# RWKV scan: the triangular inverse of a 64-step chunk in seven products, two small VectorE steps in GpSimd's queue

## The reference, cut to what matters

```
for each head, direction and chunk:   (I - A) s = x
A  = strictly triangular 64x64 product of decayed keys, scaled by 1 / |k|^2
y  = decayed r S + masked products with v and s;   S = decayed S + k^T v + b^T s
```

## Time and profile before

| what | value |
|---|---|
| median of 3 runs | 4044.05 us |
| range of the runs | 4041.13 to 4046.62 us |
| span of the profiled execution | 4039.7 us |
| TensorE busy in the span | 3727.0 us (92%) |
| VectorE, ScalarE, GpSimd busy | 2360.8, 1204.0, 1321.7 us |

### The profile page before, as it was taken

The page is one execution under the profiler, slowest core; times in us unless marked ns, Lnnn a source line. Parts: engine busy times, 40 slices in busy tenths (PEclk is TensorE's granted clock), DMA queues, the critical chain, the costliest instruction groups (busy, mean ns, idle before and its releaser), DMA issues. The chain is left out here.

```text
span 4039.7 us, 81581 instructions
## 1 busy us (share of the span) xinstructions
PE 3727.0 (92%) x32706; PEld 2683.2 (66%) x32706; DVE 2360.8 (58%) x3864; ACT 1204.0 (30%) x2668; POOL 1321.7 (33%) x1020
## 2 busy tenths in 40 slices
PE   8888999898999999899999997998999999899887
PEld 6667878657787898777344444874999998733333
DVE  4568882545985445565444445767888776623333
ACT  3352222344222322331111112224455454111112
POOL 4443444434445364573000000431555453000000
PEclk9999999999999999999999999999999999899999
DMA  4114542303554122345999995356333234589997
GB/s 128 56 53 170 184 157 93 104 1 105 178 187 146 66 96 75 99 138 228 404 420 420 420 420 212 134 177 201 88 89 91 78 93 147 199 366 422 421 421 316
DMA packets 231204, 787.80 MB, mean 195 GB/s; under 512 B 56008, under 2 KB 64024, under 8 KB 171136
## 3 DMA queue, kind: packets, MB, share of 16 engines
q1 hardware_dynamic: 225008, 764.12, 50.9%
q0 software_dynamic: 5328, 19.40, 1.2%
q10 hardware_dynamic: 576, 0.09, 0.0%
HBM read 736.15 MB, written 47.38 MB: 194 GB/s over the span
## 5 line engine op out<-in xcount | busy, mean ns | idle before, releaser
L2887 POOL DMA_INDIRECT moe0e_xg<-moe_h,moe_first_rows x20 | 18.9, 947 | 546.3 <-DVE moe_first_rows L3044 540.5
L3011 ACT ACT_TABLE_LOAD x32 | 41.1, 1283 | 519.2 <-PE moe1e_p_u L2957 262.4
L373 POOL TENSOR_TENSOR gmi_w_lo<-gmi_rows_w,gmi_w_hi 128x512 fp32r<-128x512 f32 x64 | 120.2, 1878 | 159.8 <-ACT gmi_w_hi L415 159.8
L3960 PE MATMUL scan_bank<-scan_T,scan_off 64*64 64x64 f32 x3840 | 159.4, 220 | 8.5 <-issue 5.7
L373 POOL TENSOR_TENSOR p_w_lo<-p_rows_w,p_w_hi 128x512 fp32r<-128x512 f32 (+3 forms) x88 | 113.5, 1291 | 159.9 <-ACT p_w_hi L415 159.9
L2887 POOL DMA_INDIRECT moe1e_xg<-moe_h,moe_first_rows x17 | 16.0, 940 | 451.0 <-DVE moe_first_rows L3044 444.4
L1159 POOL TENSOR_TENSOR f0u_w_lo<-f0u_w,f0u_w_hi 128x1024 fp32r<-128x1024 f32 x42 | 115.0, 2757 | 137.6 <-ACT f0u_w_hi L1175 137.6
L1159 POOL TENSOR_TENSOR f1u_w_lo<-f1u_w,f1u_w_hi 128x1024 fp32r<-128x1024 f32 x42 | 114.3, 2742 | 137.5 <-ACT f1u_w_hi L1175 137.5
L1227 DVE SCALAR_TENSOR_TENSOR f0u_ada<-hT,condition,f0u_ada 128x512 f32<-128x512 f32 x168 | 148.2, 949 | 16.4 <-DMA hT<-in_ada_w_dram 15.9
L1227 DVE SCALAR_TENSOR_TENSOR f1u_ada<-hT,condition,f1u_ada 128x512 f32<-128x512 f32 x168 | 140.5, 903 | 20.5 <-DMA hT<-in_ada_w_dram 20.0
L2984 PE MATMUL moe0e_p_y<-moe_ring,moe0e_gatedT 128*64 128x512 f32 x608 | 137.6, 605 | 7.8 <-ACT moe0e_gatedT L3013 7.8
(11 more groups left out here) (903 smaller groups left out, 11529.7 us busy)
## 6 DMA issues: line engine op xcount, KB each, us to landing
moe_ring<-in_moe_w_down_dram SPq DMA_DIRECT2D x140, 1024.0 KB, 18.0
gm_uT<-in_moe_w_gu_dram SPq DMA_DIRECT2D x111, 1024.0 KB, 16.6
moe_ring<-in_moe_w_gu_dram SPq DMA_DIRECT2D x102, 1024.0 KB, 24.7
walk_memory<-in_moe_w_gu_dram SPq DMA_DIRECT2D x60, 1024.0 KB, 24.4
hT<-in_ada_w_dram SPq DMA_DIRECT2D x48, 1024.0 KB, 6.8
f0u_w<-in_ffn_w_gate_up_dram SPq DMA_DIRECT2D x22, 1024.0 KB, 4.8
f1u_w<-in_ffn_w_gate_up_dram SPq DMA_DIRECT2D x22, 1024.0 KB, 4.8
gmi_rows_w<-in_ga_w_in_dram SPq DMA_DIRECT2D x64, 256.0 KB, 2.7
```

The costliest lines, as they stand in the source:

```text
L373: nc.gpsimd.tensor_tensor(w_lo[t % 2][:, 0:width], w[t % RAW][:, 0:width], w_hi[t % 2][:, 0:width], ALU.subtract).then_inc(w_lo_made, 1)
L2887: pool.indirect_dma_start(xg[:], None, H.h, bass.IndirectOffsetOnAxis(rows[:, 0:1], 0)).then_inc(gathered, 16)
L3011: nc.scalar.activation(sg[:], p_g[:], ACT.Silu).then_inc(silu_ready, 1)
L3960: mm = nc.tensor.matmul(out[r], lhsT[r], rhs[r], start=start, stop=stop, skip_group_check=True)
```

## The change

The inverse is reorganised. A 64x64 triangle consists of two 32x32 blocks on the diagonal and a piece that joins them. Inside the blocks R is now built as (I + W^8)(I + W^4)(I + W^2)(I + W) times the first join, W being a product of the remaining joins with that first inverse. Since R is then zero outside the two diagonal blocks, its 64 columns are added ("folded") to 32, and the power W (64 columns) and the folded R (32 columns) lie side by side in `WR`, so that one matmul of 96 columns gives both the square and the product.

There are PRODUCTS = 7 stages of 3 group products: FIRST (64 columns), three squaring stages (96 columns), LAST_POWER (32 columns, the folded R alone), OUTER and FINAL (64 columns) for the outer join. `UNITS` lists 30 units: a squaring product is two units of half a group each, the others are one unit each. The walk parts and the factor steps are placed on units as they were on group products.

GpSimd's queue is now, per head: for each group `full` and `off`, then three folds (128x128), three outer pieces, `split_block`, `add_shift`, the factors `km` and `kh`, and then three unfolds (`r_full`, 128x256, which wait for VectorE's LAST_POWER additions), and `eed`. VectorE gives up `split_block` and `add_shift`.

```diff
-LEVELS = 5
+BLOCK_BITS = 5
+PRODUCTS = 7
...
+    FIRST, LAST_POWER, OUTER, FINAL = 0, 4, 5, 6
+    UNITS = [(n, part) for n in range(NI) for part in ((0, 4),) * (n // NG not in (1, 2, 3)) + ((0, 2), (2, 4)) * (n // NG in (1, 2, 3))]
...
-        off = [sb(f"off{n}", [P, 4, CH]) for n in range(NZ)]
-        Z = [sb(f"Z{n}", [P, 4, CH]) for n in range(2)]
+        off, off_outer = (sb(n, [P, STEPS, CH]) for n in ("off", "off_outer"))
+        Z = sb("Z", [P, STEPS, CH])
+        WR = sb("WR", [P, STEPS, CH + CH // 2])
+        full = sb("full", [P, STEPS, CH])
...
@@ gpsimd @@
-                    for n in range(NZ):
...
-                        nc.gpsimd.tensor_tensor(off[n][:], strict(u, g), over4(join[:, l + 1, :]), ALU.mult).then_inc(s["off_ready"], 1)
+                        nc.gpsimd.tensor_tensor(full[:, g4, :], strict(u, g), over4(join[:, 0, :]), ALU.mult).then_inc(s["r_joined"], 1)
+                        nc.gpsimd.tensor_tensor(off[:, g4, :], strict(u, g), over4(join[:, 1, :]), ALU.mult).then_inc(s["off_ready"], 1)
+                    for g in range(NG):
+                        g4 = slice(4 * g, 4 * g + 4)
+                        pool.wait_ge(s["r_ready"], h * NG + g + 1)
+                        nc.gpsimd.tensor_tensor(WR[:, g4, folded], full[:, g4, 0:CH // 2], full[:, g4, CH // 2:CH], ALU.add).then_inc(s["r_folded"], 1)
+                    for g in range(NG):
+                        nc.gpsimd.tensor_tensor(off_outer[:, 4 * g:4 * g + 4, :], strict(u, g), over4(join[:, 2, :]), ALU.mult).then_inc(s["outer_ready"], 1)
+                    split_block(h)
+                    add_shift(h)
                     if ahead is not None:
                         factors(ahead)
+                    for g in range(NG):
+                        g4 = slice(4 * g, 4 * g + 4)
+                        pool.wait_ge(s["r_added"], h * ADDED + adds_through(LAST_POWER * NG + g))
+                        nc.gpsimd.tensor_tensor(by_block(full[:, g4, :]), WR[:, g4, folded].rearrange("p c (o t) -> p c o t", o=1).broadcast_to([P, 4, 2, CH // 2]),
+                                                join[:, 3, :].rearrange("p (q o t) -> p q o t", q=1, o=2).broadcast_to([P, 4, 2, CH // 2]), ALU.mult).then_inc(s["r_full"], 1)
+                    if ahead is not None:
+                        end_decays(ahead)
@@ scalar @@
+                    for k, (n, (first, end)) in enumerate(UNITS):
+                        if n // NG in (FIRST, OUTER):
+                            copy_z(n)
+                        if squares(n) and end == 4:
+                            copy_power(n)
+                        walk_part(walk, k - 1)
+                        if ahead is not None and k % 2 == 0 and k:
+                            factor_part(ahead, k // 2 - 1)
@@ vector @@
                     add_bonus()
-                    split_block()
-                    add_shift()
...
+                    for k, (n, (first, end)) in enumerate(UNITS):
+                        if end == 4:
+                            if n and squares(n - 1):
+                                add_product(n - 1)
+                                turn_product(n - 1)
+                            if not squares(n):
+                                add_product(n)
+                            if n and not squares(n - 1):
+                                turn_product(n - 1)
                         if ahead is not None:
+                            factor_part(fc, ahead, k)
@@ tensor @@
+                        for q in range(first, end):
+                            j = n % NG * 4 + q
+                            if stage == FIRST or stage == OUTER:
+                                mm = mmul(one(n)[:, q, :], stationary[:, j, :], T[:, j, :])
+                            elif squares(n):
+                                mm = mmul(wide(n)[:, q], stationary[:, j, :], WR[:, j, :])
+                            elif stage == LAST_POWER:
+                                mm = mmul(narrow(n)[:, q, :], stationary[:, j, :], WR[:, j, folded])
+                            else:
+                                mm = mmul(one(n)[:, q, :], stationary[:, j, :], full[:, j, :])
...
+                    for k, (n, (first, end)) in enumerate(UNITS):
+                        product(n, first, end)
+                        walk_part(k - 1)
```

More of the change, by code:

```diff
@@ new lines, in turn, with add_product @@
+                    def turn(out, of):
+                        V.transpose(out, of).then_inc(s["t_made"], 1)
+                    def add_product(n):
+                        g4 = chunks(n)
+                        if n // NG == FIRST or n // NG == OUTER:
+                            return
+                        if squares(n):
+                            dve.wait_ge(s["z_copied"], h * COPIED + copies_through(n))
+                        else:
+                            dve.wait_ge(s["inv_ready"], h * NI + n + 1)
+                        if squares(n):
+                            if n // NG == 1:
+                                dve.wait_ge(s["r_folded"], h * NG + n % NG + 1)
+                            V.tensor_tensor(WR[:, g4, folded], WR[:, g4, folded], wide(n)[:, :, folded], ALU.add).then_inc(s["r_added"], 1)
+                        elif n // NG == LAST_POWER:
+                            V.tensor_tensor(WR[:, g4, folded], WR[:, g4, folded], narrow(n), ALU.add).then_inc(s["r_added"], 1)
+                        else:
+                            if h >= 2 and n % NG == 0:
+                                dve.wait_ge(s["sa_ready"], (h - 1) * STEPS)
+                            V.tensor_tensor(R[u][:, g4, :], full[:, g4, :], one(n), ALU.add).then_inc(s["r_added"], 1)
@@ L4149, in rwkv_tables @@
     joins = []
-    for l in range(LEVELS + 1):
+    for l in range(BLOCK_BITS + 1):
         m = 1 << l
```

169 lines of the change are left out of this document (85 added, 84 removed).

## The result

The changed kernel takes 4001.53 us (median of 4 runs, 4000.18 to 4004.44), the kernel before, on the same chip, 4045.14 (4041.13 to 4046.62). The ratio is 0.9892, 95% interval 0.9878 to 0.9906.

A forecast was written before the change was run, and what follows sets the result against it. TensorE's stream was taken to bound heads 1 to 15. -2.4 + 0.5 + 0.95, some -1.0 us a head, gave 15 us; with head 0's 2.5, 17.5 less: 4026.5 us, range 4004 to 4046.

The forecast's parts named there:

- Holes of that kind come in most heads and I expect them to stay: TensorE's inverse stage: holes of a little over a microsecond, put down to "issue", were expected to remain after the change.
- TensorE's work, -2.4 a head: Inverse stage: products cost 11.6 us instead of 14.0, with 41.5 ns a row for 96 columns and 29.2 for narrower.
- Hops +0.5: Walk parts waiting for ScalarE's copy of the part before: 0.5 us a head more, bounds 0 and 1.2.
- unfold +0.95: TensorE waiting before OUTER for VectorE's addition, GpSimd's unfold and VectorE's transpose: 0.45, 0.25 and 0.25 us a head.
- The two terms of 0.14 and 0.45 us: 0.14: extra hop shortfall where a finished power's copy stands in front; 0.45: TensorE's wait for the first unfolded group.
- Head 0, 2.5 us: Head 0 gains 2.5 us (0 to 4): split and shift leave VectorE, 1.9; shorter VectorE work 2; unfold's trip takes 1.5.
- The pair stage "at 10.2 as before": A sign to check: each head's pair stage, before its inverse stage, keeps its 10.2 us.
- Everything is covered, 4004: Rival: walk parts hide the unfold's round trip and the hops, so all 40 us comes: 4004; chance 0.15.
- The hops don't hold: Denies the rival that ScalarE's chain sets the squaring units and half of the 2.4 us is lost: 4044; chance 0.16.
- Neither slow one: Two rivals: unfold at 1.8 us each, 4068, chance 0.07; 96 columns costing what 128 do, 4055, chance 0.05.
- One engine at a time in SBUF: Rival: VectorE and GpSimd block each other; rk step waits for second unfold, third comes 0.35 us later: 4031; chance 0.17.
- its second row: Evidence cited against the SBUF rival: the unit-matrix addition, SBUF alone, took 465 ns beside the masks, 416 at best.

The follow-up runs named there:

- dense stream back: Kernel after with every 96-column matmul issued as one of 64 and one of 32 columns: 4057.31 us, ratio 1.0016 to the kernel before.
- bytes away: Kernel before with factor and cumulative loads from head 2 on cut to one chunk's columns or one edge: 4028.72 us, ratio 0.9953.
- bytes doubled: Kernel before with each factor and cumulative load from head 2 on followed by a copy to unread HBM scratch: 4064.48 us, ratio 1.0051.

## Why the prediction was wrong, point by point

- **"Holes of that kind come in most heads and I expect them to stay": the step that failed.** 18.6 of the 40.5 - 17.5 = 23 us missing between the spans. The row was read, and labelled "issue", which is no cause. Had I numbered the instructions of the queue, the holes would have stood at equal places modulo 256, and then the change touches them: it makes TensorE's instructions fewer (826 rows in the window of an inverse stage become 683) and longer. The runs show the fetch in its place. TensorE waits at the ends of its blocks of 256 instructions, 22.1 us in heads 1 to 14 of before and 4.2 in after; dense stream back, 32.5 us there and 4057 in all; bytes away, 20 us less; bytes doubled, 21 more.
- **TensorE's work, -2.4 a head: right.** 41.6 and 28 ns for 41.5 and 29.2.
- **Hops +0.5, unfold +0.95: right in size** (0.44, as a difference, and 0.86). The two terms of 0.14 and 0.45 us in their working don't come out of the rows that stand beside them (0.26 in front of a hop of 0.49 or 0.58 that has 0.56; 2.05 less 1.63 is 0.42). Net -1.14 for -1.0 a head.
- **Head 0, 2.5 us: too small**, 4.65 between these two traces. 1.58 of that is its pair stage (10.62 and 9.04), and no work of the change lies there: in before the granted clock was 0.50 (the 1.2 GHz level) over its first 5 us, in after 1.00, by the windows below. In the other traces this stage takes 8.60 to 10.68 us. Of the 3.08 in the inverse stage the move is worth 0.4 to 0.7 (I had 1.9 as the split and the shift stood there), the rest is the shorter work of TensorE and VectorE, which I had put at 2 less 1.5. As the clock differs between such stages, I leave the split at that. Before, then after:

```profile
2812.16:2817.16 5.00, 5.00 (x64) 5.00 (x66) 2.21 (x6) 0.63 (x1) 2.09 (x2) 0.50 1.02 253
```
```profile
2810.73:2815.00 4.27, 4.27 (x86) 3.84 (x88) 3.22 (x9) 0.63 (x1) 2.78 (x3) 1.00 1.05 246
```

- **The pair stage "at 10.2 as before": right**, 10.19.
- **Rivals.** "Everything is covered, 4004" has the nearest number for a wrong reason: nothing is covered, the stage has 2.6 us of waiting. The hops don't hold. Neither slow one came: the unfold takes 727 ns, 96 columns don't cost what 128 do. One engine at a time in SBUF: the mechanism is there, and I had its second row wrong. The additions of 465 ns do wait for the mask (0.19 us left of it, and 0.28 behind it), and the rk step waits for the second unfold, as this rival said. But only 0.28 us of that unfold are left when it starts, so it loses 0.12 us and not 0.35, and the third OUTER product comes no later: 0.86 of waiting in all where this rival needed 1.3.
- **The range** had its lower end at the most that the steps could give. It had no term for a loss that is there today and might go.

## What to carry to other kernels

A hole inside a run of equal matmuls that no semaphore releases is a thing to number before it is taken as given: if its distance from the next such hole is a multiple of 256 instructions, with the sequencer's own counted in, TensorE waits for its own program. In a stream of small matmuls at 29 ns a block of 256 lasts 3.7 us and its refetch about 3.5, so fewer and wider matmuls gain twice if the blocks last clearly longer by them (4.47 us for 4.10 here; 4.21 was not enough). Data transfers, which the waits never name, have a price (12 us by the traces and 20 by the medians for some 22 MB: 517 us at 83 GB/s less 505 us at 41). And before a stall is put into a forecast as constant, ask for its cause and whether the change touches it.

## What the runs showed of the hardware that I had not expected

- TensorE's instructions arrive in packets of 16,384 bytes, one for 256 instructions, 1.0 to 1.2 us long in the median (up to 1.8), and no block begins sooner than 1.15 us after the end of its packet in any trace (1.21 in before, 1.20 in after).
- These packets share the DMA engines with data: doubled loads move their start from 1.23 to 1.41 us after the last block end in the kernel before, thin loads to 1.08.
- A VectorE step with two inputs in SBUF that starts beside a running GpSimd operation ends a fixed time after that operation: 0.28 us for 128x256, 0.41 for 128x384. One with a single SBUF input is not held up (transposes of 445 ns alone and beside GpSimd).
